# Attention layer of a two-layer trunk on one core: bias and row maximum in one operation from tables, values of two pairs of heads in one product, output rows moved behind them

## The reference, cut to what matters

```python
s = einsum('bcqkgd,bcwkd->bckgqw', q, kw) * HEAD_DIM ** -0.5
dist = abs(rel)                                  # |query - key|, 0 to 127
alibi = -slopes * dist                           # one slope for each head
s = where(valid, s + alibi, NEG_INF)             # chunk 0 has no chunk before it
m = maximum(max(s, -1), sink)
p = exp(s - m)
p = p / (sum(p, -1) + exp(sink - m))
o = einsum('bckgqw,bcwkd->bcqkgd', p, vw)
return o.reshape(B, S, 1024) @ w_o
```

## Time and profile before

| | us |
|---|---|
| three runs, median (lowest to highest) | 1098.51 (1098.22 to 1098.57) |
| the profiled execution | 1098.69 |
| its span on the core | 1096.9 |
| PE busy | 1086.4 (99%) |
| DVE busy | 788.8 (72%) |
| ACT busy | 564.4 (51%) |
| attention, from the first scores to the last fillers | 613.1 to about 720.5 |
| a step of attention | 11.3 |

### The profile page before, as it was taken

How to read it: one execution, slowest core, us unless ns; L and a number is a source line. 1 busy time by engine, 2 the same in 40 slices (tenths; PEclk the granted TensorE clock), 3 DMA queues, 4 the chain that set the end, 5 groups by cost and what they waited for, 6 DMA issues and landing times.

```text
span 1096.9 us, 17600 instructions
## 1 busy us (share of the span) xinstructions
PE 1086.4 (99%) x6973; PEld 976.4 (89%) x6973; DVE 788.8 (72%) x1131; ACT 564.4 (51%) x997; POOL 27.4 (3%) x40
## 2 busy tenths in 40 slices
PE   8999999999999999999999999999999999999998
PEld 7887787889999999988889888889999999998886
DVE  5878985788988888853457798468888888863334
ACT  6377474565555555542235676555455555542223
POOL 2000000000000000001221000000000000000000
PEclk9999999999999999999999999999999999999999
DMA  6332233232333333344632201142333433342211
GB/s 205 104 100 69 77 107 116 96 96 78 99 115 116 94 101 116 121 142 122 165 104 69 48 1 39 39 116 63 94 95 115 117 93 101 116 145 101 97 42 77
DMA packets 150964, 107.25 MB, mean 98 GB/s; under 512 B 23921, under 2 KB 140769, under 8 KB 150882
## 3 DMA queue, kind: packets, MB, share of 16 engines
q1 hardware_dynamic: 150880, 106.12, 32.3%
q10 hardware_dynamic: 2, 0.00, 0.0%
HBM read 104.01 MB, written 2.10 MB: 97 GB/s over the span
## 4 chain that ended last, share of the span: by engine, by line
PE 97%; DVE 1%; ACT 1%; DMA 1%; issue 0%; SPq 0%; DVEq 0%
PE ps L1849 12%; PE ps L1847 12%; PE ps L1845 12%; PE ps L1600 11%; PE ps L1601 11%; PE ps L1604 11%; PE ps L1580 8%; PE ps L1582 8%; PE ps L1581 8%; PE ps L1776 1%; PE ps L1610 1%; PE ps L1950 1%; PE ps L1977 1%; DMA raw<-in_a_w_in 1%; PE ps L2004 1%; PE ps L2002 1%
## 5 line engine op out<-in xcount | busy, mean ns | idle before, releaser
L1051 DVE TENSOR_TENSOR w_lo<-raw,w_hi 128x1024 fp32r<-128x1024 f32 x97 | 121.7, 1258 | 164.2 <-ACT w_hi L624 164.0
L624 ACT CAST w_hi<-raw 128x1024 fp32r<-128x1024 f32 x98 | 102.2, 1047 | 167.1 <-PE ps L1604 147.4
L1845 PE MATMUL ps<-t_hi,w_hi 128*128 128x256 f32 x608 | 172.1, 283 | 0.0
L1847 PE MATMUL ps<-t_lo,w_hi 128*128 128x256 f32 x608 | 172.1, 283 | 0.0
L1849 PE MATMUL ps<-t_hi,w_lo 128*128 128x256 f32 x608 | 172.1, 283 | 0.0
L1580 PE MATMUL ps<-x_hi,w_hi 128*128 128x512 f32 (+1 forms) x384 | 137.5, 358 | 0.0
L1600 PE MATMUL ps<-w_hi,t_hi 128*128 128x512 f32 x352 | 137.2, 390 | 0.0
L1601 PE MATMUL ps<-w_lo,t_hi 128*128 128x512 f32 x352 | 137.0, 389 | 0.0
L1581 PE MATMUL ps<-x_lo,w_hi 128*128 128x512 f32 (+1 forms) x384 | 135.1, 352 | 0.0
L1582 PE MATMUL ps<-x_hi,w_lo 128*128 128x512 f32 (+1 forms) x384 | 135.0, 352 | 0.0
L1849 PE MATMUL ps<-x_hi,w_lo 128*128 128x256 f32 x456 | 129.0, 283 | 0.0
(11 more groups left out here) (229 smaller groups left out, 2200.4 us busy)
## 6 DMA issues: line engine op xcount, KB each, us to landing
raw<-in_ffn_w_gu SPq DMA_DIRECT2D x88, 512.0 KB, 4.8
raw<-in_ffn_w_down SPq DMA_DIRECT2D x44, 512.0 KB, 3.3
raw<-in_a_w_in SPq DMA_DIRECT2D x24, 512.0 KB, 4.0
raw<-in_a_w_out SPq DMA_DIRECT2D x12, 512.0 KB, 3.5
raw<-in_b_w_o SPq DMA_DIRECT2D x16, 256.0 KB, 4.0
raw_q<-in_b_w_q SPq DMA_DIRECT2D x12, 256.0 KB, 4.6
h<-in_x SPq DMA_DIRECT2D x4, 512.0 KB, 6.2
result<-h SPq DMA_DIRECT2D x3, 512.0 KB, 2.6
```

What stands on the lines that cost most here:

```text
L624: nc.scalar.copy(halves(t)[0], raw_of(t)).then_inc(w_hi_ready, 1)
L1051: v.tensor_tensor(lo, raw_of(t), hi.bitcast(F32), ALU.subtract).then_inc(w_lo_ready, 1)
L1845: nc.tensor.matmul(ps[:, b, 0:HS], w_hi[:, slot, cols], hi, start=start, stop=False, skip_group_check=True)
L1847: nc.tensor.matmul(ps[:, b, 0:HS], w_hi[:, slot, cols], lo, start=False, stop=False, skip_group_check=True)
```

## The change

1. *Bias from tables, and the maximum with it.* POOL writes one table of slope times distance for each head (`alibi`, 16 times 128x192), four before it scales the query weights and twelve after the transposes of the boundary ahead of attention, into memory of `work` and `junk`. `biased` is now eight `tensor_tensor_reduce`, one for each token block and head, that add the table and leave the maximum of the row and the sink in `sm`. The reduction over 1536 elements and the maximum with the sink go.
2. *No first chunk for block 0.* Scores, exponentials and divisions of token block 0 run over two chunks of keys, not over three with one masked (`FIRST_CHUNK`).
3. *Values of two pairs at once.* `p_hi` and `p_lo` hold two steps side by side, and `values(u)` multiplies steps 2u and 2u + 1 together: up to 256 columns for each matmul, after the odd step only. The results lie in bank 3 (tokens 0 to 255) and bank 0 (256 to 511), so `turn_p` waits until bank 0 has been read, and `o_high` and `o_low` come in two halves in front of the even steps. `p_lo` takes the memory of `gpost` and `gpre`, whose loads move behind the last values.
4. *Fillers.* `values(6)` goes. The last fillers are one half of token block 0 for all four k, then the other half of block 1 and the other half of block 0.

```diff
+FIRST_CHUNK = [1, 0, 0, 0]
+
+VALUE_PARTS = [[(0, 0, 0, P), (2, 0, 0, P), (4, 1, 0, P), (6, 1, 0, P)],
+               [(1, 0, 0, P), (3, 0, 0, CHUNK), (3, 1, CHUNK, P), (5, 1, 0, P), (7, 1, 0, CHUNK)]]
...
-    p_hi = sb("p_hi", [P, 2, TC, P], F32R)
-    p_lo = sb("p_lo", [P, 2, TC, P], F32R)
+    p_hi = sb("p_hi", [P, 2, TC, 2, P], F32R)
...
+    p_lo = sb("p_lo", [P, 2, TC, 2, P], F32R, at["gpost"])
...
+    alibi_01 = sb("alibi_01", [P, 4, WIN], F32, end_b)
+    end_b += 4 * 4 * WIN
+    alibi_26 = sb("alibi_26", [P, 10, WIN], F32, at["work"])
+    alibi_7 = sb("alibi_7", [P, 2, WIN], F32, at["junk"])
...
+        def turned_p(odd):
+            return bank(odd).rearrange("p (c n) -> p c n", n=P)
+
+        def two_outputs(half):
+            return bank(3 if half == 0 else 0).rearrange("p (m n) -> p m n", m=2)
...
-                if m == 0:
-                    load_gains(2)
+            sp.wait_ge(o_ready, PAIRS_H)
+            load_gains(2)
...
+            def alibi(m):
+
+                for g in range(2):
+                    slope = -(2.0 ** (-8.0 * (m + PAIRS_H * g + 1) / HEADS))
+                    ins = nc.gpsimd.tensor_scalar(alibi_of(m, g), dist[:, :], slope, 0.0, ALU.mult, ALU.add)
+                ins.then_inc(alibi_ready, 1)
+
+            pool.wait_ge(params_ready, 1)
+            pool.wait_ge(hidlo_ready, 2 * HID_RING)
+            alibi(0)
+            alibi(1)
...
+            pool.wait_ge(turned, 2 * TC)
+            pool.wait_ge(std_ready, pre_at(1, TC - 1) + 1)
+            for m in range(2, PAIRS_H):
+                alibi(m)
...
-                        nc.scalar.activation(s_sb[:, m % 2, j, :, g, :], s_sb[:, m % 2, j, :, g, :], ACT.Exp,
+                        part = s_sb[:, m % 2, j, FIRST_CHUNK[j]:, g, :]
+                        nc.scalar.activation(part, part, ACT.Exp,
                                              bias=sm[:, m % 2, 1, n:n + 1], accum_out=sm[:, m % 2, 3, n:n + 1])
...
                 act.wait_ge(pt_ready, 2 * m + odd + 1)
-                n = 4 * P - odd * CHUNK
-                nc.scalar.copy(p_hi[:, odd, :, :].rearrange("p c n -> p (c n)")[:, 0:n], ps[:, odd, 0:n])\
-                    .then_inc(phi_ready, 1)
-
-            def o_high(m):
-                act.wait_ge(o_ready, m + 1)
-                nc.scalar.copy(o_hi[:, m, :], bank(3)).then_inc(ohi_ready, 1)
+                nc.scalar.copy(p_hi[:, odd, :, m % 2, :], turned_p(odd)).then_inc(phi_ready, 1)
+
+            def o_high(u, half):
+                act.wait_ge(o_ready, 2 * u + half + 1)
+                nc.scalar.copy(o_hi[:, 2 * u:2 * u + 2, half * HS:half * HS + HS], two_outputs(half)).then_inc(ohi_ready, 1)

             for m in range(-1, PAIRS_H):
-                if m >= 1:
-                    o_high(m - 1)
+                if m >= 2 and m % 2 == 0:
+                    o_high(m // 2 - 1, 1)
+                    o_high(m // 2 - 1, 0)
...
+                then(v.tensor_copy(dist[:, :], dist_i[:, :]))
+                then(v.tensor_scalar(dist_n[:, :], dist[:, :], -1.0, None, ALU.mult))
+                then(v.tensor_tensor(dist[:, :], dist[:, :], dist_n[:, :], ALU.max))
+                v.memset(dist[0:CHUNK, 2 * CHUNK:], MASKED)
+                v.memset(dist[CHUNK:P, 0:CHUNK], MASKED).then_inc(params_ready, 1)
...
             def biased(m, pair):

                 dve.wait_ge(s_ready, 2 * m + pair + 1)
-                js = slice(2 * pair, 2 * pair + 2)
-                for g in range(2):
-                    head = m + PAIRS_H * g
-                    src = ps[:, 4 + 2 * pair + g, 0:2 * WIN].rearrange("p (c w) -> p c w", w=CHUNK)
-                    into = s_sb[:, m % 2, js, :, :, :].rearrange("p j c g w -> p (j c) g w")[:, :, g, :]
-                    away = dist[:, pair:pair + 2, :].rearrange("p j (c w) -> p (j c) w", w=CHUNK)
-                    ins = v.scalar_tensor_tensor(out=into, in0=away, scalar=slopes[:, head:head + 1], in1=src,
-                                                 op0=ALU.mult, op1=ALU.add)
+                dve.wait_ge(alibi_ready, m + 1)
+                b = m % 2
+                for j in (2 * pair, 2 * pair + 1):
+                    c0 = FIRST_CHUNK[j]
+                    for g in range(2):
+                        cols = slice((j % 2) * WIN + c0 * CHUNK, (j % 2) * WIN + WIN)
+                        n = 2 * j + g
+                        ins = v.tensor_tensor_reduce(
+                            out=s_sb[:, b, j, c0:, g, :],
+                            in0=ps[:, 4 + 2 * pair + g, cols].rearrange("p (c w) -> p c w", w=CHUNK),
+                            in1=alibi_of(m, g)[:, c0 * CHUNK:].rearrange("p (c w) -> p c w", w=CHUNK),
+                            scale=1.0, scalar=sinks[:, m, j, g:g + 1], op0=ALU.add, op1=ALU.max,
+                            accum_out=sm[:, b, 0, n:n + 1])
                 ins.then_inc(s_read, 1)

             def row_max(m):
                 b = m % 2
                 dve.wait_ge(s_read, 2 * (m + 1))
-                then(v.tensor_reduce(sm[:, b, 0, :].rearrange("p (j g) -> p j g", g=2),
-                                     s_sb[:, b, :, :, :, :].rearrange("p j c g w -> p j g c w"), AX.XY, ALU.max))
                 sink = sinks[:, m, :, :].rearrange("p j g -> p (j g)")
-                then(v.tensor_tensor(sm[:, b, 0, :], sm[:, b, 0, :], sink, ALU.max))
                 v.tensor_scalar(sm[:, b, 1, :], sm[:, b, 0, :], -1.0, None, ALU.mult)
                 v.tensor_tensor(sm[:, b, 2, :], sink, sm[:, b, 0, :], ALU.subtract).then_inc(max_ready, 1)
...
-                n = 4 * P - odd * CHUNK
-                v.tensor_tensor(p_lo[:, odd, :, :].rearrange("p c n -> p (c n)")[:, 0:n], ps[:, odd, 0:n],
-                                p_hi[:, odd, :, :].rearrange("p c n -> p (c n)")[:, 0:n].bitcast(F32), ALU.subtract)\
-                    .then_inc(plo_ready, 1)
-
-            def o_low(m):
-                dve.wait_ge(ohi_ready, m + 1)
-                v.tensor_tensor(o_lo[:, m, :], bank(3), o_hi[:, m, :].bitcast(F32), ALU.subtract).then_inc(olo_ready, 1)
+                v.tensor_tensor(p_lo[:, odd, :, m % 2, :], turned_p(odd), p_hi[:, odd, :, m % 2, :].bitcast(F32),
+                                ALU.subtract).then_inc(plo_ready, 1)
+
+            def o_low(u, half):
+
+                dve.wait_ge(ohi_ready, 2 * u + 1 + (half if u == PAIRS_H // 2 - 1 else 1 - half))
+                into = slice(2 * u, 2 * u + 2), slice(half * HS, half * HS + HS)
+                v.tensor_tensor(o_lo[:, into[0], into[1]], two_outputs(half), o_hi[:, into[0], into[1]].bitcast(F32),
+                                ALU.subtract).then_inc(olo_ready, 1)
...
             for m in range(PAIRS_H):
+                if m >= 2 and m % 2 == 0:
+                    o_low(m // 2 - 1, 1)
                 divided(m)
-                if m >= 1:
-                    o_low(m - 1)
+                if m >= 2 and m % 2 == 0:
+                    o_low(m // 2 - 1, 0)
                 if m == 0:
                     row_max(1)
                 elif m + 1 < PAIRS_H:
@@ -1549,7 +1586,8 @@
                     split_lo(T_Q + 3 + 2 * m)
                 elif m + 2 < PAIRS_H:
                     split_lo(T_Q + 5 + m)
-            o_low(PAIRS_H - 1)
+            o_low(PAIRS_H // 2 - 1, 0)
+            o_low(PAIRS_H // 2 - 1, 1)
...
@@ -1966,6 +2005,7 @@
                 pe.wait_ge(p1_ready, m + 1)
                 if m > 0:
                     pe.wait_ge(plo_ready, 2 * m)
+                    pe.wait_ge(olo_ready, m // 2 * 2)
...
-            def values(m):
-
-                if m > 0:
-                    pe.wait_ge(olo_ready, m)
+            def values(u):
+
+                if u > 0:
+                    pe.wait_ge(olo_ready, 2 * u)
                 for odd in range(2):
-                    pe.wait_ge(plo_ready, 2 * m + odd + 1)
-                    for i in range(TC):
-                        c = 2 * i + odd
-                        n = min(P, S - c * CHUNK)
-                        into = ps[:, 3, c * CHUNK:c * CHUNK + n]
-                        nc.tensor.matmul(into, v_hi[:, c, :], p_hi[:, odd, i, 0:n], start=c == 0, stop=False,
+                    pe.wait_ge(plo_ready, 4 * u + 3 + odd)
+                    for c, half, lo, hi in VALUE_PARTS[odd]:
+                        col = c * CHUNK + lo - half * HS
+                        into = two_outputs(half)[:, :, col:col + hi - lo]
+                        first, last = lo == 0 and c in (0, 4), odd == 1 and c in (3, 7) and (c, half) != (3, 1)
+                        i = c // 2
+                        nc.tensor.matmul(into, v_hi[:, c, :], p_hi[:, odd, i, :, lo:hi], start=first, stop=False,
                                          skip_group_check=True)
-                        nc.tensor.matmul(into, v_hi[:, c, :], p_lo[:, odd, i, 0:n], start=False, stop=False,
+                        nc.tensor.matmul(into, v_hi[:, c, :], p_lo[:, odd, i, :, lo:hi], start=False, stop=False,
```

(44 more changed lines are left out.)

15 lines of the change are left out of this document (6 added, 9 removed).

## The result

The changed kernel takes **1099.91 us** at the median of 19 runs (1097.61 to 1102.79), the kernel before 1098.30 (1098.05 to 1099.96, 20 runs). The ratio is 1.0016 [1.0009, 1.0022]: slower by 1.6 us, where 1.4 us of gain were forecast. The single runs lie 5.2 us apart, those of the kernel before 1.9. (A twentieth run took 6069 us, which nothing on record explains; it is left out.) The profiled execution took 1101.75 for a span of 1100.0, so it is 3.06 above that of before.

The account below looks back on a forecast made before the run. PE, busy 99% of the span, was taken as the bound. Terms -8.7 + 4.5 + 1.0 + 1.4 + 0.6 - 0.2 = -1.4 us from 1098.51 gave 1097.1 us, range 1095.5 to 1100.4.

Parts of the forecast that it names:

- Scores behind the even steps: PE waits for q_lo before the scores after steps 0, 2 and 4, 1.5 us each: plus 4.5 us.
- Transposes of the even steps: PE waits 2.0 us, 0.60 before, for both o_low ahead of step 6's transposes: plus 1.4 us.
- rival 3: DVE becomes the bound, with a fused pair at 0.53 us and late divisions: +1.9, 1100.4 us, chance 0.20.
- Values, -8.7: Merged value matmuls on PE: four blocks of 3.2 us replace eight totalling 21.3, minus 8.7 us.
- rival 4: 256 columns in two pieces cost two products: values gain 0.9 in place of 8.7, 1104.9 us, chance 0.05.
- The fused operation, +1.0: On DVE, eight pairs (main part plus accumulator read) at 0.405 us delay step 0's denominators: plus 1.0 us, 0.5 at 0.34.
- rival 2: Accumulator read hides (pair 0.34) and the boundary's transfers land in time: -2.5, 1096.0 us, chance 0.25.
- Boundary, +0.6: At the boundary after attention, a later released tile delays the first transpose: up to 0.8, taken as plus 0.6 us.
- Rival 5: The waits don't come because q_high and q_low are made in time: 1092.8 us, chance 0.05.
- the floor of 1.4: Least wait before the even steps' scores: last query matmul's end and two copies that nothing can hide, 1.4 us.
- What was to be seen: Profile signs: 3.2 us merged blocks, score waits about 1.5, first transposes 1, seventh 2, fused pairs 0.4 apart.

Follow-up runs that it names:

- the interleaved fillers: The changed kernel with merged values moved behind the next even step's scores, its last fillers now interleaved so tile slots free earlier: 1095.30 us.
- the late values: The changed kernel reordered: merged values behind the next even step's scores, all queries ahead of the transposes, query casts ahead of the probabilities': 1095.66 us.
- filled kernels: The changed kernel with dummy matmuls in PE's waits: all four 1097.12 us, score waits only 1098.12, last transposes' wait only 1099.01, all by half 1096.68.
- the last kernel: The kernel measured at 1092.80 us, with the first half of the scores no longer waiting for the last bias piece: 1090.23 us, ratio 0.9923.
- only the last was filled: The changed kernel with dummy products only in the 2.0 us wait ahead of the last transposes, none ahead of the scores: 1099.01 us.
- half filled kernel: The changed kernel with three dummy products ahead of each even step's scores and four ahead of the last transposes: 1096.68 us.
- the kernel of 1092.80: The kernel measured at 1095.30 us, with copies, bias pieces, a weight's low part and a filler reordered against its remaining waits: 1092.80 us, ratio 0.9948.
- the scores filled: The changed kernel with dummy products in the three waits ahead of the scores only, the wait before the last transposes left empty: 1098.12 us.

## Why the prediction was wrong

**The step that failed** is the price of PE's waits, in the terms "Scores behind the even steps" and "Transposes of the even steps". Their number, place, releaser and length were right (4.2 us measured for 4.5, 1.4 for 1.4). But they were priced at their own length. Behind a wait of 1.4 or 2.0 us the granted clock can fall to half, and the matmuls of 512 columns that follow cost 0.43 in place of 0.23: 1.6 us for a fall (3.0 for the longest seen), 4.5 us in the profiled execution, 2.8 at the median of the runs (1099.91 - 1097.12). No rival had it, and it is the whole distance from the forecast of 1097.1 to the result. The measured time does lie in the range of 1095.5 to 1100.4, but that is luck: the upper end came from rival 3, whose mechanism did not come. The prediction also took 2.2 us as the least that a measurement can tell, and the runs tell less: 1.0 to 2.4 us slower, by the interval.

**Values, -8.7:** right, -8.6. Two pieces of 128 columns cost like 256 in one; rival 4 is out. **The fused operation, +1.0:** 0.5. The read hides all but wholly (pair 0.34, the low end), so rival 3, DVE as the bound, did not come; the first half of rival 2 did. **Transposes, +1.4:** right. **Boundary, +0.6:** 1.3, more than the 0.8 given as the most. The later freeing of the slots was the cause named, and the interleaved fillers confirm it for the late values; in the changed kernel it was not tested. Its profile has 1.3, those of the filled kernels 0.7 to 1.0, and why is open. The two errors of size cancel, by luck, and so the kernel with its waits filled stands at 1097.12. **Rival 5** (no waits) needed the floor of 1.4 to be wrong. It was right for this order of work, and the last kernel shows that another order gets below it.

**What was to be seen** was right line by line, and yet the forecast failed: every line asked for was one of waits and lengths. The clock stands in the same rows of the windows (the earlier trace rows has it: 1.00), and I had read it as a constant of the kernel. It was one as long as PE never waited there for more than 0.6 us.

The Trainium skill, TensorE: Matmul & The Clock Gate, has a section, A second HAM failure mode: psum-queue depth-cycling, by which an engine that often idles a little between groups of matmuls makes its clock swing between the levels. The runs here agree in kind, with 1.6 to 3.0 us for a swing. The rule that the section HAM oscillation takes as the abstract one would have allowed idle gaps longer than any of these; the 0.50 measured behind a gap of 1.40 decides against it.

**Still open:** why a given wait brings a fall and the next of the same length does not (two of three in the changed kernel's profile, one of three where only the last was filled), and where the limit of length lies. Length alone does not decide. The profile of the first kernel of the late values (1095.66 at the median) has waits of 0.63 and 0.74, ending 2.3 us apart, and one of 1.65, and its clock stays at 1.00 all through attention; that of the next (1095.30) has 0.60, 0.74 and 1.65 at the same places, and falls behind both. The half filled kernel's waits of 0.7 to 0.84 brought no fall in its profile, though one of its runs reached 1098.91; in the kernel of 1092.80 a wait of 0.86 brought a fall (0.79 over the 8 us around it), in the last one a wait of 0.9 none. And not every slow run goes with the clock: the fused operation alone took 1100.69 us once at 1.000.

## What to carry to other kernels

A wait put on a matmul engine that never waited before is not worth its length only: look at what stands behind it, and add the difference between the two clock levels for the matmuls there, as a case with its own chance. Work taken out of a saturated engine pays only if what it covered has been moved as well; otherwise dummy matmuls in the gap can be better than nothing (7 us of work removed made a kernel 1.8 us slower, and 18 dummy matmuls put in gave back 3.45). And two halves of a change need not add up: here the one was worth -0.5 us alone and 5.5 beside the other.

## What was not expected of the hardware

- The granted clock fell behind waits of 1.4 us, not in the wait but 1.7 us after it, and stood at 0.50 for 3.4 us. The scores in between kept their distance of 0.11 because the clock was still at 1.00. Where it had fallen, the 512-column matmuls went from 0.23 to 0.43, the 256-column ones of the values from 0.12 to 0.21 (kernel of 1092.80, 682.82 to 683.03), and eleven transposes from 1.31 to 1.94 us (690.04 to 691.98 with the scores filled), so narrow matmuls pay too.
- The spread of a kernel's runs can go with the clock: 1096.58 us at a mean granted clock of 1.000 to 1101.03 at 0.994 for one and the same program. That it is the number of falls is likely, but each kernel has one profile.
- The fused operation with its maximum costs 0.27 us for 128 elements and 0.34 for 192 from start to start, its accumulator read of 0.08 included.
